# A decode state update in pairs on 32-row tiles of the matrix array

## The chip, the cores and the metric

The kernel runs on one core of one Trainium2 chip. The metric is the device time of one execution in microseconds (us). Engines: TensorE (PE; PEld is its weight load), VectorE (DVE), ScalarE (ACT), GpSimd (POOL), SyncE (SP).

## The reference

One layer of a hybrid decoder for a prompt of 256 tokens and for 8 decode sequences of 4 new tokens each (32 rows): 288 tokens in all, model width 2048. Around two large feed-forward parts (width 5632) stands a mixing part: one input projection, four mLSTM heads of width 256, a convolution group, one output projection. The decode sequences carry a state, a 256x256 matrix C per head and sequence:

```python
num = (jnp.einsum('bhls,bshd->blhd', s, vc)
       + jnp.einsum('blhd,bhde->blhe', qc, C) * w_inter.transpose(0, 2, 1)[..., None])
...
g_state = jnp.exp(bt[..., -1] + m - m_new)
g_keys = jnp.exp(bt[..., -1:] - bt + it - m_new[..., None])
C_new = g_state[..., None, None] * C + jnp.einsum('bhs,bshd,bshe->bhde', g_keys, kc, vc)
```

All data are float32. The change is about the second term of `C_new` for the 8 decode sequences ("batch elements"): a sum over only 4 tokens, for each of 4 heads.

## The kernel before

Everything is held feature-major: 128 features on the partitions, the 288 tokens in the free dimension. The weights come as 654 pieces of 128x1024 floats through four slots. Each piece is split into a rounded high half (`whi`, by ACT at L910) and a rest (`wlo`, by DVE at L1330 or POOL at L1860), and each 128x128 block of it makes three matmuls over 288 columns (L473 to L475). A piece is 8 blocks, so 24 matmuls; two pieces make an output tile of the input projection. Every engine runs a list of steps p, one for each piece of the mixing part, and the small work of the heads is hung onto these steps by hand: `head_part(h, k)` runs in step p = `KEYS_AT[h]` + k, with `KEYS_AT` = (8, 30, 54, 78), and on PE `between(p, j)` is called after block j of piece p. At even steps DVE first evicts a tile of the projection (`evict`, which waits for the end of a piece), then does the head parts, then its share of the splits.

What touches the change, for each head:

- ACT (k = 8) copies the 32 decode columns of K and V four times side by side (`kv4`), PE turns them to token-major (`to_token_major`), so 128 rows hold the 32 decode rows four times.
- The four copies carry the four products of two rounded halves each: ACT (k = 10) writes the high halves of `v4` and `k4`, DVE (k = 11, L1674 and L1678) turns some row groups into the rests. One 128-row matmul then adds high*high, high*rest, rest*high and rest*rest.
- ACT (k = 12, 13, L1189) writes `vm`, eight copies of `v4`, each with all rows but those of one batch element set to zero.
- `update_memory(h, b)` on PE makes, for one batch element, two matmuls (L744) of a 128x128 block of `k4` with the 256 columns of `vm[b]`, into bank 7 or 4 by turns. There are eight such places per head, three blocks apart, at `updates`, counted from step 16 + `LATE[h]`, with `LATE` = (2, 0, 0, 3).
- DVE (L1737) adds each result to the old state in `C`: batch elements 0 to 2 in step 16, 3 and 4 in step 17, 5 to 7 in step 18 (plus `LATE[h]`); the counter `cu_evicted` tells PE that a bank is free.
- `query_memory` (L705) reads the old states: it runs on 32-column tiles of the array, four batch elements beside one another. `token_columns` (L657) makes six matmuls over 36 rows.
- `attend` (L728) waits for DVE's L1717.

Of the kernel before, what the change touches and what calls it, by code (L numbers as in the profile page):

```python
# [29 lines left out]
P = 128  # L30
# [75 lines left out]
Q_GROUP = 4  # L106

# [67 lines left out]
def hybrid_layer_kernel(nc, stream, x_in, vecs, gate_w, gate_vec, c_in, n_in, conv_in,  # L175
                        y_out, cp_out, np_out, cs_out, ns_out, m_out, conv_out):
    with ExitStack() as ctx:
# [77 lines left out]
        vm = place("vm", [P, NB, DH], F32R)  # L255
# [8 lines left out]
        mask4 = place("mask4", [P, 4, NB], F32, prod_at)  # L264
# [8 lines left out]
        mask = place("mask", [P, NB])  # L273
# [9 lines left out]
        own = bass.AP(ident, 0, [[P, P], [Q_GROUP * NT, NB // Q_GROUP], [NS + NT, Q_GROUP], [1, NT]])  # L283
# [62 lines left out]
        cap_ready, cap_added = sem("cap_ready"), sem("cap_added")  # L346
        turn_ready, sums_ready = sem("turn_ready"), sem("sums_ready")
# [26 lines left out]
        def four(ap):  # L374

            return ap.unsqueeze(2).broadcast_to([P, DC, P // NS, NS])
# [79 lines left out]
        def _(pe):  # L456
# [237 lines left out]
            def query_memory(h):  # L694
# [7 lines left out]
                for r in range(NB // Q_GROUP):  # L702
                    for c in range(DC):
                        for j in range(Q_GROUP):
                            mm = pe.matmul(bank[4][NS * j:NS * (j + 1), 0:DH], qw[:, c, r, :],  # L705
                                           C[:, r * Q_GROUP + j, c, :], start=(r + c == 0),
                                           stop=(r == NB // Q_GROUP - 1 and c == DC - 1), skip_group_check=True,
                                           tile_position=(0, NS * j))
# [73 lines left out]
            updates = {(16, 1): 0, (16, 4): 1, (16, 7): 2, (17, 2): 3, (17, 5): 4, (18, 0): 5, (18, 3): 6, (18, 6): 7}  # L782

            def between(p, j):


                for h in range(H):
# [13 lines left out]
                    b = updates.get((k - LATE[h], j))  # L801
                    if b is not None:
                        update_memory(h, b)
# [98 lines left out]
        def _(act):  # L902
# [185 lines left out]
            def gate_rows():  # L1088

                act.wait_ge(args_ready, 1)  # L1090
                for k in range(2):
# [3 lines left out]
                act.activation(rowg[:, SEQ:SEQ + P].rearrange("h (j i) -> h j i", i=NS),  # L1095
                               g_arg[:, 0:NS].unsqueeze(1).broadcast_to([H, P // NS, NS]), ACT.Exp).then_inc(rows_ready, 1)
# [3 lines left out]
                act.dma_start(row_copy[:, R_GK:ROWS], rowg[:, 0:TOK]).then_inc(rows_stored, 16)  # L1100
# [25 lines left out]
            def head_part(h, k):  # L1126
# [9 lines left out]
                if h == 0 and k == 6:  # L1136

                    act.wait_ge(rows_stored, 32)
# [15 lines left out]
                if k == 8:  # L1154

                    act.wait_ge(tile_evicted, tile_of(h, "v1") + 1)
                    for n in range(2):
                        last = act.activation(kv4[:, n, :, :].rearrange("p c (j t) -> p c j t", j=P // NS),
                                              four(qkvo[:, 1 + n, :, SEQ:TOK]), ACT.Copy)
                    last.then_inc(kv4_ready, 1)  # L1160
                if k == 10:
# [8 lines left out]
                    act.activation(v4[:, :], bank[7][:, 0:DH], ACT.Copy, scale=col[:, 5, h:h + 1])  # L1170
                    act.activation(k4[:, :], bank[7][:, DH:2 * DH], ACT.Copy).then_inc(dec_hi, 1)
# [12 lines left out]
                if k in (12, 13):  # L1184
# [3 lines left out]
                    for b in range(4 * (k - 12), 4 * (k - 11)):  # L1188
                        act.activation(vm[:, b, :], v4[:, :].bitcast(F32), ACT.Copy, scale=mask[:, b:b + 1])\  # L1189
# [131 lines left out]
        def _(dve):  # L1321
# [238 lines left out]
            dve.tensor_reduce(mask[:, :], mask4[:, :, :].rearrange("p j b -> p b j"), AX_X, ALU.add)\  # L1560
# [33 lines left out]
            four_dec = [H, P // NS, NB, NT]  # L1594
# [573 lines left out]
```

## Time and profile before

| | |
|---|---|
| median of 3 runs | 2156.44 us (2156.44 to 2157.05) |
| the profiled execution | 2157.24 us |
| its span, first to last instruction | 2155.5 us |
| PE busy | 2149.3 us (100%), 16278 matmuls |
| DVE, ACT, POOL busy | 972.9, 895.1, 961.7 us |
| granted TensorE clock | 1.000 |

The span is 1.7 us short of the execution's own time. The busy time of an engine is the union of its instructions; the recorded duration of a matmul overlaps those of its neighbours, so the pace is read from starts, not from durations.

### The profile page before, as it was taken

How to read it: one execution, taken by the hardware profiler on the slowest of the kernel's cores; microseconds unless marked ns; L12 is line 12 of the kernel's file. 1: busy time of each engine (PE TensorE's matmuls, PEld its weight loads, DVE VectorE, ACT ScalarE, POOL GpSimd, SP SyncE). 2: the span in 40 equal slices, each digit the busy share in tenths (PEclk: the TensorE clock that was granted, in tenths of full speed). 3: DMA queues.
4: the chain of work that ended last, by engine and by line, in shares of the span. 5: the costliest groups of instructions: out<-in, count | busy, mean ns of one | idle time of the engine just before them, and what ended most of it. 6: DMA issues, size and time to landing. Idle time of an engine off the chain costs nothing.

```text
span 2155.5 us, 41798 instructions
## 1 busy us (share of the span) xinstructions
PE 2149.3 (100%) x16278; PEld 2138.5 (99%) x16278; DVE 972.9 (45%) x1406; ACT 895.1 (42%) x1159; POOL 961.7 (45%) x563
## 2 busy tenths in 40 slices
PE   9999999999999999999999999999999999999999
PEld 9999999999999999999999999999999999999998
DVE  6533432223434224987659738533432223333323
ACT  6434333333343335644345446433333333333443
POOL 1444443334444445466756332444443334444444
PEclk9999999999999999999999999999999999999999
DMA  7454555455555554656656544545455545554653
GB/s 249 165 168 163 165 166 172 159 165 168 167 164 162 170 169 146 208 191 229 239 191 226 194 160 148 172 160 171 156 172 168 167 157 170 162 172 157 210 164 129
DMA packets 104692, 376.63 MB, mean 175 GB/s; under 512 B 11640, under 2 KB 15868, under 8 KB 103584
## 3 DMA queue, kind: packets, MB, share of 16 engines
q1 hardware_dynamic: 97632, 349.00, 49.0%
q10 hardware_dynamic: 6848, 26.37, 3.5%
q8 instruction: 62, 1.02, 0.2%
q14 instruction: 22, 0.18, 0.0%
q0 software_dynamic: 128, 0.07, 0.0%
HBM read 360.21 MB, written 15.18 MB: 174 GB/s over the span
## 4 chain that ended last, share of the span: by engine, by line
PE 99%; DVE 1%; issue 0%; ACT 0%; POOL 0%; DVEq 0%; POOLq 0%
PE bank L475 30%; PE bank L473 30%; PE bank L474 30%; PE bank L528 1%; PE bank L535 1%; PE bank L539 1%; PE bank L833 1%; PE bank L835 1%; PE bank L834 1%; PE bank L546 0%; PE bank L744 0%; PE bank L770 0%; PE bank L687 0%; DVE wlo L1330 0%; DVE prod L1636 0%; PE bank L728 0%
## 5 line engine op out<-in xcount | busy, mean ns | idle before, releaser
L1860 POOL TENSOR_TENSOR wlo<-raw,whi 128x1024 fp32r<-128x1024 f32 x331 | 796.6, 2408 | 850.5 <-ACT whi L910 770.7
L473 PE MATMUL bank<-xh,whi 128*128 128x288 f32 x3344 | 992.1, 297 | 0.0
L474 PE MATMUL bank<-xl,whi 128*128 128x288 f32 x3344 | 988.3, 296 | 0.0
L475 PE MATMUL bank<-xh,wlo 128*128 128x288 f32 x3344 | 986.4, 295 | 0.0
L910 ACT ACTIVATE whi<-raw 128x1024 fp32r<-128x1024 f32 x652 | 687.3, 1056 | 604.8 <-PE bank L475 560.8
L1330 DVE TENSOR_TENSOR wlo<-raw,whi 128x1024 fp32r<-128x1024 f32 x323 | 467.7, 1449 | 771.2 <-ACT whi L910 769.9
L473 PEld LDWEIGHTS bank<-xh,whi 128*128 128x128 f32 x3344 | 630.2, 188 | 2.4 <-issue 2.2
L475 PEld LDWEIGHTS bank<-xh,wlo 128*128 128x128 f32 x3344 | 629.8, 188 | 0.0
L474 PEld LDWEIGHTS bank<-xl,whi 128*128 128x128 f32 x3344 | 628.7, 188 | 0.2
L475 PE MATMUL bank<-hh,wlo 128*128 128x288 f32 x1408 | 417.4, 296 | 0.0
L473 PE MATMUL bank<-hh,whi 128*128 128x288 f32 x1408 | 416.1, 296 | 0.0
L474 PE MATMUL bank<-hl,whi 128*128 128x288 f32 x1408 | 410.5, 292 | 0.0
L474 PEld LDWEIGHTS bank<-hl,whi 128*128 128x128 f32 x1408 | 268.4, 191 | 0.0
L473 PEld LDWEIGHTS bank<-hh,whi 128*128 128x128 f32 x1408 | 264.5, 188 | 0.0
L475 PEld LDWEIGHTS bank<-hh,wlo 128*128 128x128 f32 x1408 | 263.8, 187 | 0.0
L1883 POOL TENSOR_TENSOR scr<-scr 128x288 f32<-128x288 f32 x88 | 74.7, 849 | 208.7 <-ACT scr L999 208.7
L1003 ACT ACTIVATE hh<-scr 128x288 f32 (+1 forms) x88 | 39.1, 444 | 275.6 <-DVE scr L1468 275.6
L999 ACT ACTIVATE scr<-scr 128x288 f32<-128x288 f32 x88 | 39.2, 445 | 220.7 <-DVE scr L1447 220.7
L1447 DVE TENSOR_TENSOR scr<-bank,rstd 128x288 f32<-128x288 f32 x176 | 80.3, 456 | 77.1 <-PE bank L475 72.3
L1624 DVE SCALAR_TENSOR_TENSOR bank<-upad,vec,bank 128x256 f32<-128x256 f32 x232 | 92.8, 481 | 0.1
L1873 POOL TENSOR_TENSOR ssq<-ssq,sq 128x288 f32<-128x288 f32 x45 | 36.5, 812 | 79.3 <-ACT sq L1060 54.2
L1470 DVE TENSOR_TENSOR hl<-scr,hh 128x288 f32 (+1 forms) x88 | 40.3, 458 | 64.0 <-ACT hh L1003 64.0
(265 smaller groups left out, 1271.4 us busy)
## 6 DMA issues: line engine op xcount, KB each, us to landing
raw<-stream SPq DMA_DIRECT2D x654, 512.0 KB, 3.5
C<-c_in ACTq DMA_DIRECT2D x4, 2048.0 KB, 8.2
cs_out<-C ACTq DMA_DIRECT2D x4, 2048.0 KB, 7.9
late_kv<-late ACTq DMA_DIRECT2D x1, 2048.0 KB, 13.5
y_out<-x_res SPq DMA_DIRECT2D x7, 288.0 KB, 2.2
bc<-row_copy ACTq DMA_DIRECT2D x4, 448.0 KB, 8.6
conv_out<-upad ACTq DMA_DIRECT2D x4, 302.0 KB, 5.0
upad<-conv_in ACTq DMA_DIRECT2D x4, 272.0 KB, 3.4
```

What stands on the lines that cost most here:

```text
L473: pe.matmul(out, wh, mov_hi[:, k, :], start=first, stop=False)
L474: pe.matmul(out, wh, mov_lo[:, k, :], start=False, stop=False)
L475: return pe.matmul(out, wl, mov_hi[:, k, :], start=False, stop=last)
L910: act.activation(whi[:, g % SLOTS, :], raw[:, g % SLOTS, :], ACT.Copy).then_inc(hi_ready, 1)
L999: act.activation(scr[:, 2, :], scr[:, f % 2, :], ACT.Sigmoid).then_inc(sig_ready, 1)
L1003: act.activation(hh[:, k, :], scr[:, 4, :], ACT.Copy).then_inc(h_hi, 1)
L1330: dve.tensor_tensor(wlo[:, g % SLOTS, :], raw[:, g % SLOTS, :], whi[:, g % SLOTS, :].bitcast(F32), ALU.subtract).then_inc(lo_ready[g % SLO ...
L1447: ins = dve.tensor_tensor(out, src, rstd[:, :], ALU.mult)
L1470: dve.tensor_tensor(hl[:, k, :], scr[:, 4, :], hh[:, k, :].bitcast(F32), ALU.subtract)\
L1624: ins = dve.scalar_tensor_tensor(out=out, in0=up_prompt(j, SEQ, k), scalar=w, in1=acc, op0=ALU.mult, op1=ALU.add)
L1860: pool.tensor_tensor(wlo[:, g % SLOTS, :], raw[:, g % SLOTS, :], whi[:, g % SLOTS, :].bitcast(F32), ALU.subtract).then_inc(lo_ready[g % SL ...
L1883: pool.tensor_tensor(scr[:, 5 + f % 2, :], scr[:, f % 2, :], scr[:, 2, :], ALU.mult)\
```

## The change

The decode rows are ordered by batch element, then copy, then token: the 16 rows of a batch element (4 copies x 4 tokens) lie together, and a group of 32 rows holds two batch elements, 2g (even, r = 0) and 2g + 1 (odd, r = 1). The state update of a batch element then needs the 32 rows of its group only. `vm` has two versions, one with the odd and one with the even 16-row halves set to zero. Two batch elements of neighbouring groups (on different banks) are issued beside one another on 32-row tiles of the array, at four places per head.

```diff
+PAR = NB // Q_GROUP
+COPIES = P // NS
+UPDATE_ORDER = (0, 2, 1, 3, 4, 6, 5, 7)
...
-            def update_memory(h, b):
-
-                if b < 2:
-                    pe.wait_ge(den_ready if b == 0 else qc_evicted, h + 1)
+            def update_memory(h, n):
+
+                if n:
+                    pe.wait_ge(cu_evicted, NB * h + 2 * n)
                 else:
-                    pe.wait_ge(cu_evicted, NB * h + b - 1)
-                pe.wait_ge(vm_ready, NB * h + b + 1)
-                out = bank[4 if b % 2 else 7]
+                    pe.wait_ge(den_ready, h + 1)
+                    pe.wait_ge(qc_evicted, h + 1)
+                    pe.wait_ge(vm_ready, PAR * (h + 1))
                 for c in range(DC):
-                    mm = pe.matmul(out[:, c * DH:(c + 1) * DH], k4[:, c * P:(c + 1) * P], vm[:, b, :],
-                                   start=True, stop=True)
-                mm.then_inc(cu_done, 1)
+                    for b in UPDATE_ORDER[2 * n:2 * n + 2]:
+                        g, r = divmod(b, PAR)
+                        own_rows = slice(NS * g, NS * (g + 1))
+                        mm = pe.matmul(bank[4 if g % 2 else 7][:, c * DH:(c + 1) * DH], k4[own_rows, c * P:(c + 1) * P],
+                                       vm[own_rows, r, :], start=True, stop=True, tile_position=(NS * g, 0))
+                        if c == DC - 1:
+                            mm.then_inc(cu_done, 1)
...
-            updates = {(16, 1): 0, (16, 4): 1, (16, 7): 2, (17, 2): 3, (17, 5): 4, (18, 0): 5, (18, 3): 6, (18, 6): 7}
+            updates = {(16, 1): 0, (16, 7): 1, (17, 5): 2, (18, 3): 3}
...
-                act.dma_start(row_copy[:, R_GK:ROWS], rowg[:, 0:TOK]).then_inc(rows_stored, 16)
+                act.dma_start(row_copy[:, R_GK:R_GK + SEQ], rowg[:, 0:SEQ]).then_inc(rows_stored, 16)
+                act.dma_start(row_copy[:, R_GK + SEQ:ROWS].rearrange("h (b t) -> h b t", t=NT),
+                              in_copies(rowg[:, SEQ:SEQ + P])[:, :, 0, :]).then_inc(rows_stored, 16)
...
                     for n in range(2):
-                        last = act.activation(kv4[:, n, :, :].rearrange("p c (j t) -> p c j t", j=P // NS),
-                                              four(qkvo[:, 1 + n, :, SEQ:TOK]), ACT.Copy)
+                        for c in range(DC):
+                            last = act.activation(in_copies(kv4[:, n, c, :]), copied(
+                                qkvo[:, 1 + n, c, SEQ:TOK].rearrange("p (b t) -> p b t", t=NT)), ACT.Copy)
...
-                    act.activation(v4[:, :], bank[7][:, 0:DH], ACT.Copy, scale=col[:, 5, h:h + 1])
-                    act.activation(k4[:, :], bank[7][:, DH:2 * DH], ACT.Copy).then_inc(dec_hi, 1)
+                    act.wait_ge(colv_ready, 1)
+                    act.activation(v4[:, :], bank[7][:, 0:DH], ACT.Copy, scale=colv[:, 1, h:h + 1])
+                    act.activation(k4[:, :], bank[7][:, DH:2 * DH], ACT.Copy, scale=side[:, 1, 0:1]).then_inc(dec_hi, 1)
...
-                if k in (12, 13):
+                if k == 12:
...
-                    for b in range(4 * (k - 12), 4 * (k - 11)):
-                        act.activation(vm[:, b, :], v4[:, :].bitcast(F32), ACT.Copy, scale=mask[:, b:b + 1])\
+                    for r in range(PAR):
+                        act.activation(vm[:, r, :], v4[:, :].bitcast(F32), ACT.Copy, scale=mask[:, r:r + 1])\
                            .then_inc(vm_ready, 1)
...
+            dve.wait_ge(low_ready, 2)
+            dve.tensor_reduce(side[:, 0, 0:1], low16[:, :], AX_X, ALU.add)
+            link(dve.tensor_reduce(side[:, 0, 1:2], low8[:, :], AX_X, ALU.add))
+            dve.tensor_scalar(side[:, 1, :], side[:, 0, :], -2.0, 1.0, ALU.mult, ALU.add).then_inc(side_ready, 1)
...
+                    dve.wait_ge(side_ready, 1)
+                    for n in range(2):
+                        last = dve.tensor_scalar(colv[:, n, :], col[:, 5, :], side[:, n, 1:2], None, ALU.mult)
+                    last.then_inc(colv_ready, 1)
+                    dve.wait_ge(colv_ready, 1)
                 if k == 11:
 
                     dve.wait_ge(dec_hi, h + 1)
-                    for r in (NS, 3 * NS):
-                        dve.scalar_tensor_tensor(out=v4[r:r + NS, :], in0=bank[7][r:r + NS, 0:DH],
-                                                 scalar=col[r:r + NS, 5, h:h + 1], in1=v4[r:r + NS, :].bitcast(F32),
-                                                 op0=ALU.mult, op1=ALU.subtract)
-                    half = slice(2 * NS, P)
-                    dve.tensor_tensor(k4[half, :], bank[7][half, DH:2 * DH], k4[half, :].bitcast(F32), ALU.subtract)\
-                       .then_inc(dec_lo, 1)
+                    dve.scalar_tensor_tensor(out=v4[:, :], in0=bank[7][:, 0:DH], scalar=colv[:, 0, h:h + 1],
+                                             in1=v4[:, :].bitcast(F32), op0=ALU.mult, op1=ALU.add)
+                    dve.scalar_tensor_tensor(out=k4[:, :], in0=bank[7][:, DH:2 * DH], scalar=side[:, 0, 0:1],
+                                             in1=k4[:, :].bitcast(F32), op0=ALU.mult, op1=ALU.add).then_inc(dec_lo, 1)
...
-                for b in ((0, 1, 2), (3, 4), (5, 6, 7))[first] if 0 <= first < 3 else ():
-                    dve.wait_ge(cu_done, NB * h + b + 1)
-                    src = bank[4 if b % 2 else 7][:, :]
+                for n in ((0, 1), (2, 3), (4, 5, 6, 7))[first] if 0 <= first < 3 else ():
+                    dve.wait_ge(cu_done, NB * h + n + 1)
+                    b = UPDATE_ORDER[n]
+                    src = bank[4 if b // PAR % 2 else 7][:, :]
```

The new row order is carried through the rest: the masks (POOL's selects, two more memsets and four more selects for `low8` and `low16`, and DVE's three operations on `side` above), the layout of `own`, `cap` and `turn`, the choice of `C[:, PAR * j + r]` in `query_memory`, and DVE's query weights (k = 12), where the one multiply into `qw` becomes one for the even and one for the odd batch elements.

## Rows read from the trace of the kernel before

**Rows 1.** The page: busy time of the engines, granted clock, the chain that ended last

```profile
PE 2149.3 (100%) x16278; PEld 2138.5 (99%) x16278; DVE 972.9 (45%) x1406; ACT 895.1 (42%) x1159; POOL 961.7 (45%) x563
...
PEclk9999999999999999999999999999999999999999
...
PE 99%; DVE 1%; issue 0%; ACT 0%; POOL 0%; DVEq 0%; POOLq 0%
```

**Rows 2.** Instructions of L744: durations (min/median/max, ns), first and last start, shapes

```profile
L744 PE MATMUL bank<-vm,k x64: 274/279/285, 950.4 to 1214.4; 128*128 128x256 f32 x64
```

**Rows 3.** PE's timeline, second head: start, us, engine, line, shapes, count

```profile
1030.03 0.30 PE L473 MATMUL bank<-xh,whi 128*128 128x288 f32 x1
...
1030.43 0.39 PE L744 MATMUL bank<-vm,k 128*128 128x256 f32 x2
1030.66 0.29 PE L473 MATMUL bank<-xh,whi 128*128 128x288 f32 x1
...
1031.86 0.40 PE L744 MATMUL bank<-vm,k 128*128 128x256 f32 x2
```

**Rows 4.** Timeline of all engines around the column-tiled `query_memory`, first head

```profile
941.32 0.29 PE L475 MATMUL bank<-xh,wlo 128*128 128x288 f32 x1
941.54 1.93 PE L705 MATMUL bank<-C,qw 128*32 128x256 f32 x32
...
943.41 0.40 PE L473 MATMUL bank<-xh,whi 128*128 128x288 f32 x1
...
943.65 0.29 PE L474 MATMUL bank<-xl,whi 128*128 128x288 f32 x1
```

**Rows 5.** Timeline of all engines around the 36-row matmuls of `token_columns`

```profile
904.69 0.29 PE L475 MATMUL bank<-xh,wlo 128*128 128x288 f32 x1
...
904.91 0.74 PEld L657 LDWEIGHTS bank<-ident,both 36*128 36x128 f32 x6 [0.16 <-issue]
904.91 0.83 PE L657 MATMUL bank<-ident,both 36*128 36x8 f32 x6
...
905.67 0.40 PE L473 MATMUL bank<-xh,whi 128*128 128x288 f32 x1
...
905.91 0.29 PE L474 MATMUL bank<-xl,whi 128*128 128x288 f32 x1
```

**Rows 6.** Weight loads of one round of `query_memory` (PEld's timeline)

```profile
941.79 0.13 PEld L705 LDWEIGHTS bank<-C,qw 128*32 128x32 f32 x4
```

**Rows 7.** Timeline at the start of step 18, first head (piece starts at 957.19)

```profile
957.19 0.30 PE L473 MATMUL bank<-xh,whi 128*128 128x288 f32 x1
...
957.39 0.46 DVE L1540 TENSOR_TENSOR scr<-bank,rstd 128x288 f32<-128x288 f32 x1
```

**Rows 8.** Timelines of ACT, POOL and DVE before and in step 18, second head

```profile
1026.39 1.06 ACT L910 ACTIVATE whi<-raw 128x1024 fp32r<-128x1024 f32 x1 [0.84 <-PE bank L475]
...
1027.53 2.41 POOL L1860 TENSOR_TENSOR wlo<-raw,whi 128x1024 fp32r<-128x1024 f32 x1 [1.19 <-ACT whi L910]
...
1030.94 0.46 DVE L1525 TENSOR_TENSOR scr<-bank,rstd 128x288 f32<-128x288 f32 x1 [0.76 <-POOL upad L1995]
...
1031.32 0.74 DVE L1737 SCALAR_TENSOR_TENSOR C<-C,bc,bank 128x512 f32<-128x512 f32 x1
```

**Rows 9.** Timeline of a wait of PE for DVE, second head

```profile
1019.21 0.48 DVE L1717 SCALAR_TENSOR_TENSOR sq<-bank,turn,vs 128x256 f32<-128x256 f32 x1
...
1019.81 0.19 PEld L728 LDWEIGHTS bank<-st,vtok 128*128 128x128 f32 x1 [0.40 <-issue]
```

**Rows 10.** Groups by line and shape, 880 to 1260 us: count, busy us, mean ns, idle

```profile
L1189 ACT ACTIVATE vm<-v,mask 128x256 fp32r<-128x256 f32 x32 | 13.6, 495 | 1.8 <-DVE k L1678 1.8
...
L1687 DVE TENSOR_TENSOR qw<-qkvo,bc 128x64 f32<-128x64 f32 x4 | 2.5, 626 | 0.1
```

**Rows 11.** Timeline, first head: DVE's sums and PE's `denominators` that wait for them

```profile
935.18 0.18 DVE L1712 TENSOR_TENSOR scr<-bank,qwn 128x32 f32<-128x32 f32 x1
...
936.60 0.38 PE L716 MATMUL bank<-st,ones 128*128 128x128 f32 x2
```

More of the change, by code:

```diff
@@ L254, in hybrid_layer_kernel @@
         assert gwt_at + 4 * XC * GATE_M <= vm_at + 4 * NB * DH
-        vm = place("vm", [P, NB, DH], F32R)
+        vm = place("vm", [P, PAR, DH], F32R, vm_at)
+        low_at = gwt_at + 4 * XC * GATE_M
+        low8 = place("low8", [P, P // 8], F32, low_at)
+        low16 = place("low16", [P, P // 16], F32, low_at + 4 * P // 8)
+        assert low_at + 4 * (P // 8 + P // 16) <= vm_at + 4 * NB * DH
+        arena[0] += 4 * NB * DH
         late_kv = place("late_kv", [P, H, 4, DH], F32, xl_at)
@@ L263, in hybrid_layer_kernel @@
         assert upad_at + 4 * 7 * TOK <= arena[0]
-        mask4 = place("mask4", [P, 4, NB], F32, prod_at)
+        mask4 = place("mask4", [P, Q_GROUP, PAR], F32, prod_at)
         rows = place("rows", [H, R_GK], F32, prod_at)
@@ L272, in hybrid_layer_kernel @@
         ntmp = place("ntmp", [P, DC, NB])
-        mask = place("mask", [P, NB])
+        mask = place("mask", [P, PAR])
+        side = place("side", [P, 2, 2])
+        colv = place("colv", [P, 2, H])
         qwn = place("qwn", [P, DC, NS])
@@ L370, in compact, with copied, in_copies @@
             return row[:, SEQ:TOK].rearrange("h (b t) -> h b t", b=NB)
[L374 to L376 removed]
+        def copied(ap):
+            return ap.unsqueeze(2).broadcast_to([ap.shape[0], NB, COPIES, NT])
+        def in_copies(ap):
+            return ap.rearrange("p (b j t) -> p b j t", j=COPIES, t=NT)
         g_f, g_az, g_e, g_arg, g_wi = (gt[:, k, :] for k in range(5))
@@ L800, in between @@
                         attend(h)
-                    b = updates.get((k - LATE[h], j))
-                    if b is not None:
-                        update_memory(h, b)
+                    n = updates.get((k - LATE[h], j))
+                    if n is not None:
+                        update_memory(h, n)
                 if (p, j) == (MIX_FROM, 3):
@@ L1684, in head_part @@
                         dve.wait_ge(num_done, 3 * h)
[L1685 to L1694 removed]
+                    n = Q_GROUP * NT
+                    for r in range(PAR):
+                        w = bc[:, h % 2, R_WI:R_GK].rearrange("p (g r t) -> p r g t", r=PAR, t=NT)[:, r, :, :].unsqueeze(1)
+                        last = dve.tensor_tensor(
+                            qw[:, :, r, n * r:n * (r + 1)].rearrange("p c (g t) -> p c g t", t=NT),
+                            qkvo[:, 0, :, SEQ:TOK].rearrange("p c (g r t) -> p c r g t", r=PAR, t=NT)[:, :, r, :, :],
+                            w.broadcast_to([P, DC, Q_GROUP, NT]), ALU.mult)
+                    link(last)
+                    for r in range(PAR):
+                        old = n0[:, h, :, :].rearrange("p c (g r) -> p c r g", r=PAR)[:, :, r, :].unsqueeze(3)\
+                            .broadcast_to([P, DC, Q_GROUP, NT])
+                        last = dve.tensor_tensor(
+                            qwn[:, :, :].rearrange("p c (g r t) -> p c r g t", r=PAR, t=NT)[:, :, r, :, :],
+                            qw[:, :, r, n * r:n * (r + 1)].rearrange("p c (g t) -> p c g t", t=NT), old, ALU.mult)
                     link(last)
@@ L1980, in _ @@
                     pool.wait_ge(pool_chain, 4)
+            for low, n in ((low8, 4), (low16, 8)):
+                pool.memset(low[:, :], 1.0).then_inc(pool_chain, 1)
+            pool.wait_ge(pool_chain, 6)
+            for low, n in ((low8, 4), (low16, 8)):
+                pool.affine_select(out=low[:, :], in_=low[:, :], compare_op=ALU.is_ge, fill=0.0, base=-n,
+                                   pattern=[[-2 * n, P // (2 * n)]], channel_multiplier=1).then_inc(pool_chain, 1)
+            pool.wait_ge(pool_chain, 8)
+            for low, n in ((low8, 4), (low16, 8)):
+                pool.affine_select(out=low[:, :], in_=low[:, :], compare_op=ALU.is_ge, fill=0.0, base=2 * n - 1,
+                                   pattern=[[2 * n, P // (2 * n)]], channel_multiplier=-1).then_inc(low_ready, 1)
             pool.wait_ge(xsq_sum, 2)
```

52 lines of the change are left out of this document (21 added, 31 removed).

## The prediction

> **What bounds the kernel now.** I read the page first: PE is busy in 2149.3 us of the 2155.5 us span, every slice has the full granted clock (the 2.4 GHz level), and the chain that ended last is PE for 99% [rows 1]. So a nanosecond taken from PE's list is a nanosecond of the end, one that PE waits is one too, and work taken from ACT, DVE or POOL counts only where PE waits for it. The view by line then shows what the change rebuilds: 64 matmuls of L744, 256 columns each [rows 2]. Their recorded duration, 0.28 us, is not their price: neighbours overlap. The price is read from starts: L744's pair starts at 1030.43 and the next block at 1030.66, while one block of three matmuls takes ((1031.86 - 1030.43) - 0.24) / 3 = 0.395 us [rows 3]. So a place costs 0.24 us, and all 32 places 32 x 0.24 = 7.7 us. That is all the change can save on PE, 3.8 us if every two matmuls run in the time of one: 0.18% of the kernel, under the 0.2% (4.3 us) that a measurement can tell from no change.
>
> **What a place costs after.** Four matmuls stand in one place: two rounds of two tiles. At best that is 2 x 0.12 + 0.01 = 0.25 us. But these are 32-row tiles between full-array matmuls, and two views show what such a stretch costs. `query_memory` runs on 32-column tiles: from L475's start at 941.32 to its first matmul at 941.54 it takes 0.22 us where full matmuls follow one another after 0.13, and behind it L473 holds 0.24 instead of 0.13 until L474 starts [rows 4]. The 36-row matmuls of L657, a part of the rows as in the change, show the same two numbers, 0.22 and 0.24 [rows 5]. I read it so: PE runs empty (0.09), only then loads weights, so a load that otherwise lies under the matmul before it stands in the open (0.11 for 128 columns: L657's six loads lie (0.74 - 0.19) / 5 = 0.11 apart), and the same twice at the exit. The test is the whole of L705: 0.09 + 0.03 for its first 32-column load + eight rounds + 0.02 + 0.09 + 0.11. A round is (1.93 - 0.38) / 7 = 0.22 us, with the last matmul's duration of 0.38 taken off, so 2.1 us; measured from 941.32 to 943.65, less the two ordinary spacings of 0.13, it is 2.07 [rows 4].
>
> So a new place is 0.09 (empty) + 0.11 (first weights) + 0.24 (two rounds; the second's weights load under the first) + 0.01 (second tile) + 0.09 (empty) + 0.11 (the next block's weights) = 0.65 us. Sixteen places make 10.4 us against 7.7 us: 2.7 us more. The lower bound is 16 x 0.25 = 4.0 us, so 3.7 less, if row tiles cost no change-over at all; I take the other end because both kinds of part-array work on record pay it. Whether the two tiles' loads run side by side no row shows for row tiles: for column tiles four loads lie within 0.13 - 0.11 = 0.02 us [rows 6], so I take them as parallel; one behind the other is a rival below.
>
> The Trainium skill speaks against this change in TensorEngine Tiling (Array Packing), section Key Properties: changing the tiling mode, not just the tile, drains TensorE. By that rule each of the 16 places pays a drain at both ends; the 0.09 us at each end agrees with it [rows 4, 5].
>
> **A new wait.** Each place fills both banks, so PE at place n waits until 2n results are added by DVE. The places at (16,7) and (17,5) are six blocks (2.4 us) behind the one before, and it takes 0.09 + 0.11 + 0.12 to the second round, 0.28 for its matmul [rows 2], and 1.4 us for DVE's two additions (below), 2.0 us in all: covered. The place at (18,3) is not: it needs six additions, but the fifth and sixth are in DVE's step 18, and there DVE first evicts a projection tile that ends with the piece. In the first head the piece starts at 957.19, the eviction at 957.39 (0.20 later) [rows 7]; the next operation follows after 0.38 (1030.94 to 1031.32), an addition takes 0.75 and two in a row 0.68 + 0.75 [rows 8]; and a load on PE starts 0.12 after the DVE operation it waits for ends (1019.69 to 1019.81) [rows 9]. That is 0.20 + 0.38 + 0.68 + 0.75 + 0.12 = 2.13 us after the piece started; PE comes after four blocks, 1.58. The 0.09 in which PE runs empty passes meanwhile: 2.13 - 1.58 - 0.09 = 0.46 us. Nothing is queued before it that could go ahead: every main matmul behind it waits too.
>
> In the second and third head the eviction starts 0.91 after the piece (1030.03 to 1030.94), because POOL's gating multiply is late; POOL hangs on ACT's split at 1026.39, released by the end of the piece two before [rows 3, 8]. One new place (0.65) lies before that point where two old ones (0.48) lay: POOL comes 0.17 later. The start of the piece moves by 3 x 0.65 - 5 x 0.24 = 0.75. So the lag is 0.91 + 0.17 - 0.75 = 0.33 instead of 0.20, and the wait 0.59. The bounds are 0.46 and, with the lag unmoved, 1.2. The fourth head's step 18 lies behind the projection and has no eviction ahead: no wait. Together 0.46 + 2 x 0.59 = 1.6 us.
>
> **What lies beside.** ACT makes 8 `vm` copies instead of 32, 24 x 13.6 / 32 = 10 us less [rows 10], and 16 narrower copies instead of 8; DVE makes two rests per head instead of three, two small multiplies and three reductions or scalings once; POOL two memsets and four selects, before its splits and while it waits. One more small store goes out on ACT's queue two steps before the rows are read back, and only late work, eight pieces ahead, waits for it. None of these engines sets the end; I take 0. The closest is DVE in the first head, without a gap until its sums end at 935.36; `denominators` comes at 936.60 [rows 11]. Cover: 1.24 us. The multiply into `qw` becomes two, and the mean of 626 ns for 64 columns [rows 10], beside 0.18 us for 32 columns in L1712 [rows 11], says that it sometimes stands behind something else. If the second one stands as long as a whole POOL split (2.41 [rows 8]), PE waits 2.4 - 1.2 = 1.2 us; once, in this head. I take 0 (two multiplies without a link between them pass together), and keep 1.2 for the range.
>
> **Sum.** +2.7 + 1.6 = +4.3 us on the profiled 2157.24 us (span 2155.5 and 1.7 around it), which lies 0.8 us above the median. On the median 2156.44: 2160.7 us, just at the 0.2%.
>
> **Rivals.** *Loads one behind the other* (slower): the four loads of a place take 0.11 each in the open; place 0.09 + 4 x 0.11 + 0.12 + 0.09 + 0.11 = 0.85 us, 16 of them 13.6, +5.9; the piece moves more (1.35), so the waits are 0.46 each, +1.4; 2163.7 us. For: L657's loads do queue at 0.11 [rows 5], though on one tile. Against: rows 6. It decides as soon as a load on the second tile starts 0.1 us after the first.
> *No change-over for row tiles* (not slower): places 4.0 us, -3.7; but PE then comes earlier to (18,3): lag 0.91 - 0.23 + 0.45 = 1.13, wait 1.48 twice and 0.55 once, +3.5; 2156.2 us. Against: rows 5. Without the waits too it would be 2152.7, still within 0.2%.
> The Trainium skill, TensorE: Matmul & The Clock Gate, Part 3, gives a packed set one matmul's time and about 4 ns per further tile; by that alone a round costs what it does in this rival. L705's rounds agree with it; its ends don't.
> *The wait at (18,3) is hidden*, if DVE evicts sooner than read: 2159.1 us. Against: rows 7 and 8 leave it 0.55 us too late.
>
> **Chances.** The forecast 0.56, half of it on either side of the bound; loads in a row 0.18; no change-over 0.10; hidden wait 0.10; others 0.06. Slower: 0.28 + 0.18 + 0.03 = 0.49. Same: 0.28 + 0.20 = 0.48. Faster 0.03, since no case worked out reaches it. The range 2157.0 to 2164.0 holds the forecast with 1.2 us for DVE or for late POOL, hidden waits and queued loads; it leaves out the 0.10 and the others.
>
> **What would show it.** Right: L744's successor in 16 places of four matmuls, each entered 0.22 us after the last L475 and left with 0.24 between L473 and L474; PE waiting for L1737's successor three times, at the last place of heads one to three, about half a microsecond each. Wrong: weight loads 0.11 apart on two tiles; starts of 0.13 at the entry; a wait at `denominators` in the first head; or a matmul on 32 rows that is slower than one on 128.

## The result, and the profile after

| | before | after |
|---|---|---|
| median (18 runs each) | 2156.65 us (2156.10 to 2157.21) | 2160.74 us (2160.38 to 2161.39) |
| the profiled execution, its span | 2157.24, 2155.5 us | 2161.22, 2159.5 us |
| PE busy | 2149.3 us | 2152.0 us |
| granted TensorE clock | 1.000 | 1.000 |

The change makes the kernel 4.1 us slower: ratio 1.0019, 95% interval [1.0013, 1.0026]. The interval leaves out 1, so the loss is real; its middle lies just under the 0.2% bound and its upper end above it.

The lines of the page that answer to [rows 1], from the kernel after (L488 to L490 are the main matmuls now, L762 the state update):

```profile
PE 2152.0 (100%) x16278; PEld 2136.1 (99%) x16278; DVE 974.3 (45%) x1411; ACT 887.1 (41%) x1143; POOL 961.8 (45%) x569
...
PEclk9999999999999999999999999999999999999999
...
PE 96%; DVE 2%; issue 1%; POOL 1%; ACT 0%; POOLq 0%; DVEq 0%; ACTq 0%
```

The clock is whole in every slice, as before, so no time is the clock's. ACT has 8 us less to do, and nothing comes of it. In the chain that ended last PE's share has fallen from 99% to 96%, and DVE's and POOL's have risen (1% to 2%, 0% to 1%): PE waits for them somewhere. The view of waits says where (engine, what it was to do, for whom it waited: total us, times, longest), PE of the kernel after:

```profile
PE bank L561 <- POOL ident L1965: 1.7, 1, 1.7
PE bank L762 <- DVE C L1769: 1.1, 3, 0.4
PE bank L743 <- DVE sq L1748: 0.4, 2, 0.2
PE bank L789 <- ACT rpost L1333: 0.2, 1, 0.2
PE bank L684 <- ACT cpr L1180: 0.2, 1, 0.2
```

The first, third and fourth stand in the same view of before too, with the same times. New are three waits at the update's last place (L762), which the prediction has, and one at `to_token_major` (L684), which it doesn't have.

A place of the update, in PE's timeline of the kernel after (answers to [rows 3]):

```profile
953.50 0.29 PE L490 MATMUL bank<-xh,wlo 128*128 128x288 f32 x1
953.73 0.50 PE L762 MATMUL bank<-vm,k 32*128 32x256 f32 x4
954.16 0.40 PE L488 MATMUL bank<-xh,whi 128*128 128x288 f32 x1
954.40 0.29 PE L489 MATMUL bank<-xl,whi 128*128 128x288 f32 x1
```

Read it by starts, as L705 was read in the prediction: from the last L490 to L489 behind the place it is 954.40 - 953.50 = 0.90 us (unrounded 0.893), less two ordinary spacings of 0.13 (together 0.263) is 0.63. The entry takes 0.23 (unrounded 0.224) and L488 holds 0.24: both numbers of [rows 4, 5]. All 16 places without their waits cost 0.62 to 0.63, mean 0.629.

The three waits, the one in the second head in DVE's and PE's timeline of the kernel after (its piece starts at 1031.86, answers to [rows 8]):

```profile
1032.20 0.46 DVE L1548 TENSOR_TENSOR scr<-bank,rstd 128x288 f32<-128x288 f32 x1 [2.77 <-POOL upad L2038]
1032.58 1.39 DVE L1769 SCALAR_TENSOR_TENSOR C<-C,bc,bank 128x512 f32<-128x512 f32 x2
```

```profile
1033.32 0.29 PE L490 MATMUL bank<-xh,wlo 128*128 128x288 f32 x1
1034.03 0.50 PE L762 MATMUL bank<-vm,k 32*128 32x256 f32 x4 [0.41 <-DVE C L1769]
```

DVE evicts 0.34 after the piece starts and is done with two additions at 1033.97; PE starts 0.06 later, 0.71 after its last L490 instead of 0.22. Over the three heads these places cost 0.981, 1.109 and 1.147 us, 0.35 + 0.48 + 0.52 = 1.35 above 0.629.

The fourth wait, in the first head. The chain that ended last, of the kernel after, from 903 to 918 us (start us, us, what):

```profile
909.58 2.44 DVE colv L1697
...
912.04 3.23 DVE bank L1649 x8
915.27 0.37 DVE qkvo L1557
...
915.88 0.70 ACT cpr L1180 x3
916.58 0.04 issue
916.62 0.66 PE bank L684 x4
```

A multiply of 128x4 numbers, new with the change (`colv`), takes 2.44 us there. The timelines of DVE and then POOL in the kernel after show beside what:

```profile
908.19 0.17 DVE L1692 COPY col<-bank 128x24 f32<-128x24 f32 x1
908.40 3.60 DVE L1697 TENSOR_SCALAR colv<-col,side 128x4 f32<-128x4 f32 x2
912.04 3.23 DVE L1649 SCALAR_TENSOR_TENSOR bank<-upad,vec,bank 128x256 f32<-128x256 f32 x8
915.18 0.45 DVE L1557 TENSOR_TENSOR qkvo<-bank,rstd 128x288 f32<-128x288 f32 x1
```

```profile
904.90 7.08 POOL L1892 TENSOR_TENSOR wlo<-raw,whi 128x1024 fp32r<-128x1024 f32 x3 [1.14 <-ACT whi L929]
```

POOL's three splits stand one behind the other until 911.98; DVE's two multiplies end at 912.00. Behind them come eight convolution steps and then the eviction of V (L1557 at 915.18, 3.46 us later than in the kernel before), ACT's copies `kv4` (which the trace calls `cpr`) and PE's L684. In DVE's timeline before:

```profile
911.72 0.45 DVE L1534 TENSOR_TENSOR qkvo<-bank,rstd 128x288 f32<-128x288 f32 x1
```

The place of L684 costs 1.242 us where the same place cost 0.875 before, 0.37 more.

So the 4.1 us are: places 16 x 0.629 - 32 x 0.236 = 2.5; waits at L762 1.35; L684 0.37; sum 4.2. Measured independently, by how far the main matmuls (288 columns each, counted through) start later than their counterparts in before: -0.16 us ahead of the mixing part (at 857.6) and +3.97 behind it (at 1217.1), so 4.13 us, all of it in the mixing part; behind 1217 us the shift stays at 3.97. "Shift" below means this difference. (The starts of a program's first 60 us differ from execution to execution by up to 1.2 us, so shifts are finer than times here.)

### The profile page after: what moved, and what is told of

Same layout as the page of the kernel before. It is cut to its first block, busy times and chain, and to the rows that moved or that the text cites. A ratio compares the mean times of both kernels' runs of the same rounds, so it can differ in the third digit from the quotient of the medians.

```text
span 2159.5 us, 41763 instructions
## 1 busy us (share of the span) xinstructions
PE 2152.0 (100%) x16278; PEld 2136.1 (99%) x16278; DVE 974.3 (45%) x1411; ACT 887.1 (41%) x1143; POOL 961.8 (45%) x569
## 4 chain that ended last, share of the span: by engine, by line
PE 96%; DVE 2%; issue 1%; POOL 1%; ACT 0%; POOLq 0%; DVEq 0%; ACTq 0%
PE bank L490 29%; PE bank L488 29%; PE bank L489 29%; PE bank L543 1%; PE bank L554 1%; PE bank L550 1%; PE bank L852 1%; PE bank L854 1%; PE bank L853 1%; DVE bank L1649 0%; POOL wlo L1892 0%; PE bank L561 0%; PE bank L789 0%; PE bank L702 0%; DVE wlo L1353 0%
## 5 line engine op out<-in xcount | busy, mean ns | idle before, releaser
L488 PE MATMUL bank<-xh,whi 128*128 128x288 f32 x3344 | 993.4, 297 | 0.0
L489 PE MATMUL bank<-xl,whi 128*128 128x288 f32 x3344 | 988.3, 296 | 0.0
L490 PE MATMUL bank<-xh,wlo 128*128 128x288 f32 x3344 | 986.4, 295 | 0.0
L488 PEld LDWEIGHTS bank<-xh,whi 128*128 128x128 f32 x3344 | 630.2, 188 | 4.0 <-issue 2.2
L490 PEld LDWEIGHTS bank<-xh,wlo 128*128 128x128 f32 x3344 | 629.7, 188 | 0.0
L489 PEld LDWEIGHTS bank<-xl,whi 128*128 128x128 f32 x3344 | 628.7, 188 | 0.2
L490 PE MATMUL bank<-hh,wlo 128*128 128x288 f32 x1408 | 417.4, 296 | 0.0
L488 PE MATMUL bank<-hh,whi 128*128 128x288 f32 x1408 | 416.1, 296 | 0.0
L489 PE MATMUL bank<-hl,whi 128*128 128x288 f32 x1408 | 410.5, 292 | 0.0
L489 PEld LDWEIGHTS bank<-hl,whi 128*128 128x128 f32 x1408 | 268.4, 191 | 0.0
L488 PEld LDWEIGHTS bank<-hh,whi 128*128 128x128 f32 x1408 | 264.5, 188 | 0.0
L490 PEld LDWEIGHTS bank<-hh,wlo 128*128 128x128 f32 x1408 | 263.8, 187 | 0.0
```

Source lines behind the costliest of these rows:

```text
L488: pe.matmul(out, wh, mov_hi[:, k, :], start=first, stop=False)
L489: pe.matmul(out, wh, mov_lo[:, k, :], start=False, stop=False)
L490: return pe.matmul(out, wl, mov_hi[:, k, :], start=False, stop=last)
```

## The experiments

**The timetable alone.** Kernel before, with the four places of the change, two batch elements in each, on the whole array:

```diff
-            updates = {(16, 1): 0, (16, 4): 1, (16, 7): 2, (17, 2): 3, (17, 5): 4, (18, 0): 5, (18, 3): 6, (18, 6): 7}
+            updates = {(16, 1): 0, (16, 7): 1, (17, 5): 2, (18, 3): 3}
...
-                for b in ((0, 1, 2), (3, 4), (5, 6, 7))[first] if 0 <= first < 3 else ():
+                for b in ((0, 1), (2, 3), (4, 5, 6, 7))[first] if 0 <= first < 3 else ():
```

> The kernel before, full-array matmuls and all, but with the new timetable: two batch elements at each of four places per head, into banks 7 and 4 at once, and DVE's additions in groups of 2, 2 and 4. Theory (the tiles cost 2.5 us and the new timetable's wait at the last place of heads one to three costs the rest): a place of four full matmuls takes 4 x 0.118 = 0.47 us, so places cost nothing more than before; PE still waits for the fifth and sixth addition. The wait measured after the change was the lag of the eviction plus 0.24 us; here the lag is 0.20 in the first head and about 0.7 in the next two (the piece moves by 0.23 only), so 0.4 + 0.9 + 0.9 us, and some 0.1 each for a weight load in the open: +2.3 to +2.5, 2159.0 us. Rival (all of the loss is the tiles', the timetable costs nothing): 2156.6 us. Rival (the timetable is all of it): 2160.7 us.

Measured: 2158.79 us, ratio 1.0011 [1.0002, 1.0019], shift +2.5. A place of four whole-array matmuls costs 0.475, twice 0.24, so the places cost nothing more; the whole 2.5 are waits. The first row of PE's waits, and one of the three in its timeline:

```profile
PE bank L745 <- DVE C L1739: 1.8, 3, 0.7
```

```profile
1031.74 0.29 PE L475 MATMUL bank<-xh,wlo 128*128 128x288 f32 x1
1032.78 0.74 PE L745 MATMUL bank<-vm,k 128*128 128x256 f32 x4 [0.74 <-DVE C L1739]
```

They are longer than in the change (0.74 against 0.41), as the prediction's way of counting the lag has it: its piece starts at 1030.29 and DVE evicts at 1030.96, a lag of 0.67, and 0.91 - (3 x 0.475 - 5 x 0.236) is 0.67. Places of 0.475 move the piece less than places of 0.63 do.

**The tiles alone.** The change, with DVE's fifth and sixth addition in step 17 instead of behind the eviction of step 18:

```diff
-                for n in ((0, 1), (2, 3), (4, 5, 6, 7))[first] if 0 <= first < 3 else ():
+                for n in ((0, 1), (2, 3, 4, 5), (6, 7))[first] if 0 <= first < 3 else ():
```

> The changed kernel with one edit: DVE adds the fifth and sixth result in step 17, ahead of the eviction of the projection tile, instead of behind it in step 18. Theory: the three waits at the place (18,3), 1.35 us together in the changed kernel, go; a place stays 0.63 us; 2159.4 us. Rival (the wait only moves: the eviction, now behind two more additions, is late for PE or for POOL): 2160.7 us, with a new wait of PE elsewhere.

Measured: 2159.67 us, ratio 1.0015 [1.0006, 1.0024], shift +2.9. The three waits at L762 are gone, and all 16 places cost 0.62 to 0.63. DVE itself now waits for PE's places 15 times instead of 12 (17.3 us in the mixing part instead of 10.5) and no longer for POOL at that eviction, but no new wait of PE comes of it. The wait of L684 stays. It was then taken out too, by an edit told below, in one kernel with both:

> The changed kernel with both repairs: DVE's fifth and sixth addition in step 17, and colv from the accumulator bank. Theory: what is left against the kernel before is the tiles alone, 16 x 0.63 - 32 x 0.236 = +2.5 us, and the wait at denominators in the first head that showed when to_token_major's went (0.27 us): 2159.3 us, and slower than before by its whole interval. Rival (the waits were the loss, tiles cost nothing): 2156.6 us.

Measured: 2159.56 us, ratio 1.0014 [1.0005, 1.0023], shift +2.44 (-1.24 to +1.20). PE's waits, whole:

```profile
PE bank L561 <- POOL ident L1965: 1.7, 1, 1.7
PE bank L743 <- DVE sq L1748: 0.4, 2, 0.2
PE bank L789 <- ACT rpost L1333: 0.2, 1, 0.2
```

These are before's. What is left in this profile is the places, 2.5 us: two row tiles with their change-over against two whole-array places. The median is 3.1 above before's, 0.6 more than this shift. The profiled execution was the fastest of the eleven (2158.43 to 2160.01); the others may have a wait at `denominators` as told below (0.17 to 0.46 us), which would be a part of it, but no profile of them shows it.

**What a place consists of.** The change, with each place's two rounds written twice (the second time the same results again):

```diff
-                for c in range(DC):
+                for m, c in enumerate((0, 1, 0, 1)):
...
-                        if c == DC - 1:
+                        if m == 3:
```

> The changed kernel with each round of a place done twice (the second pair of rounds writes the same results again): eight matmuls on two tiles per place instead of four. Theory (two tiles run side by side, weight loads too, and a place has a fixed price of about 0.40 us for running empty and loading in the open, twice): each further round is 0.11 to 0.12, a place 0.63 + 0.23 = 0.86 us, 16 x 0.23 = +3.7 us against the changed kernel, 0.3 less for waits that PE now comes later to: 2164.1 us. Rival (weight loads of the two tiles one behind the other): a round is 0.22, +7.0 us, 2167.7 us. Rival (the price of a place is in its matmuls, with no fixed part): a place doubles, 1.26 us, +10 us, 2170.7 us.

Measured: 2165.70 us, ratio 1.0043 [1.0030, 1.0056]. PE's timeline:

```profile
953.39 0.29 PE L490 MATMUL bank<-xh,wlo 128*128 128x288 f32 x1
953.61 0.74 PE L762 MATMUL bank<-vm,k 32*128 32x256 f32 x8
954.28 0.40 PE L488 MATMUL bank<-xh,whi 128*128 128x288 f32 x1
954.51 0.29 PE L489 MATMUL bank<-xl,whi 128*128 128x288 f32 x1
```

A place costs 0.865 (954.51 - 953.39 less 0.26), 0.237 more for two rounds of two matmuls each: a round of two tiles costs 0.118, one matmul's time. So the rest, 0.629 - 0.237 = 0.39 us, is paid once for each place whatever stands in it. The shift is 3.5 above the change's, as expected. The time is 5.0 above it. In the profile this execution is 0.5 us ahead of the change's up to the mixing part, so the last work of every engine ends 3.0 later; but the span ends 4.8 later, and the medians say that this is no accident of one execution. The other 1.8 us are the last two stores: from issue to landing they take 4.8 us (L446) and 4.5 (L1329), against 2.9 and 2.7 in the change. On one of the two queues of instructions the page counts one packet of 16 KB more than the change's page; the change's row, then this run's:

```profile
q8 instruction: 62, 1.02, 0.2%
```

```profile
q8 instruction: 63, 1.03, 0.2%
```

The last one here starts at 2160.93, among those stores, and takes 0.88 us; the change's last starts at 2140.24. That this packet holds the stores up is likely, but no run takes it away.

**Whether the tiles run side by side.** The change, with each tile's two matmuls listed together:

```diff
-                for c in range(DC):
-                    for b in UPDATE_ORDER[2 * n:2 * n + 2]:
+                for b in UPDATE_ORDER[2 * n:2 * n + 2]:
+                    for c in range(DC):
...
-                        if c == DC - 1:
-                            mm.then_inc(cu_done, 1)
+                    mm.then_inc(cu_done, 1)
```

> The changed kernel with the four matmuls of a place issued tile by tile (both halves of one batch element, then both of the other) instead of by turns. Theory (two tiles run side by side only when neighbours in PE's list lie on different tiles): first matmul alone, second and third together, fourth alone, so three rounds instead of two; a place goes from 0.63 to 0.74 us, 16 x 0.118 = +1.9 us against the changed kernel, 0.1 to 0.2 less for waits: 2162.5 us. Rival (side by side gives nothing, the places are bound by weight loads): 2160.7 us. Rival (PE reorders freely): 2160.7 us, with the same starts as in the changed kernel.

Measured: 2160.90 us, ratio 1.0020 [1.0011, 1.0030]; its shift is 0.25 above the change's, which is this profile's wait at L731 (below). A place costs 0.63 as before the edit. Starts of the single records of one place, in us, the loads on the first line of each pair:

```
the change     953.726 953.729 953.834 953.837   then L488 954.161
               953.727 953.731 953.949 953.954
tile by tile   953.760 953.766 953.868 953.875   then L488 954.198
               953.761 953.768 953.985 953.991
four tiles     950.761 950.765 950.768 950.771 950.870 950.873 950.876 950.880   then L496 951.203
               950.763 950.766 950.770 950.773 950.986 950.990 950.992 950.996
```

In the change two tiles' loads start 3 ns apart, not 0.11: the rival of loads one behind the other is out. In the edited list the second matmul belongs to the tile that is busy, and still a matmul starts 7 ns after the first, and two more 0.22 later. A record doesn't name its row tile, but it has the count that the matmul adds to `cu_done`. In the edited list the second and the fourth matmul count; in the records of all 16 places it is the third and the fourth. So the first matmuls of both tiles ran ahead of both second ones, and the place takes two rounds, 0.63 us, where the order of the list would take three, 0.75. My theory fell: the matmul that had to wait was passed over, and the other tile's was taken. Whether PE turned them round or the step that makes the program out of the kernel, no record tells. (The Trainium skill, TensorE: Matmul & The Clock Gate, Part 3, has matmuls start strictly in the order of the program; if the list reached PE as the kernel has it, the measurement differs from it, and decides.)

**The small multiplies.** The change, with the two `colv` multiplies reading their column from PSUM, where it stands anyway, ahead of its copy:

```diff
-                        last = dve.tensor_scalar(colv[:, n, :], col[:, 5, :], side[:, n, 1:2], None, ALU.mult)
+                        last = dve.tensor_scalar(colv[:, n, :], bank[7][:, 5 * H:6 * H], side[:, n, 1:2], None, ALU.mult)
```

> The changed kernel with DVE's two small multiplies into colv reading the accumulator bank instead of SBUF, and done ahead of the copy into col. Theory: in the changed kernel they took 3.60 us, where such an operation takes 0.15, because they stood behind POOL's splits; that made the last eviction of V 3.4 us late in the first head, and PE waited 0.37 us for kv4 in to_token_major. With an operand in PSUM they don't stand behind POOL: both take under 0.4 us, PE enters to_token_major after 0.13 us, 2160.4 us. Rival (the reductions into side or the four narrower copies are what is late): the wait of 0.37 us stays, 2160.7 us.

Measured: 2160.89 us, ratio 1.0020 [1.0011, 1.0028]: the same as the change; the 0.4 us that were to go did not. DVE's timeline, then POOL's, then PE's:

```profile
907.97 0.34 DVE L1694 TENSOR_SCALAR colv<-bank,side 128x4 f32<-128x4 f32 x2
...
926.16 3.85 DVE L1715 TENSOR_TENSOR qw<-qkvo,bc 128x32 f32<-128x32 f32 x2
930.04 2.39 DVE L1723 TENSOR_TENSOR qwn<-qw,n 128x32 f32<-128x32 f32 x2
```

```profile
904.67 7.10 POOL L1892 TENSOR_TENSOR wlo<-raw,whi 128x1024 fp32r<-128x1024 f32 x3 [1.12 <-ACT whi L929]
...
925.21 7.06 POOL L1892 TENSOR_TENSOR wlo<-raw,whi 128x1024 fp32r<-128x1024 f32 x3
```

```profile
936.38 0.46 PE L731 MATMUL bank<-st,ones 128*128 128x128 f32 x2
```

The pair takes 0.34 us instead of 3.60, beside the same three splits of POOL (904.67 to 911.77), and L684 costs 0.875 again, as before the change. But here the two `qw` multiplies and the two `qwn` behind them, which read SBUF alone, stand behind POOL's splits (which end near 927.6, 929.9 and 932.3; DVE's pairs end at 930.01 and 932.43), and PE waits at `denominators` (L731): the place costs 0.762 us against 0.492 without a wait, so 0.27 of the 0.37 is gone again.

The rule behind both: the Trainium skill, SBUF — State Buffer, Who interferes with whom, says that VectorE and GpSimd share a pair of SBUF ports which one instruction holds to its end; a DVE instruction with two SBUF inputs, or a copy or multiply by a scalar in a two-port mode, waits for the running GpSimd one, and one with at most one SBUF input outside those modes does not. The rows agree: 3.60 us with SBUF operands, ending with POOL's split, 0.34 with PSUM; in which mode the multiply ran no row shows.

**Whether the late rows make the wait at `denominators`.** The `colv` edit alone doesn't make that wait: the kernel with both edits contains it, and its place at L731 costs 0.493, without a wait. The wait comes where POOL's splits fall late, and POOL's order there begins when the gate rows land. The change stores its last rows with a scattered read (every fourth group of 4 values); in this edit ACT writes them once more, contiguous, and the store reads that:

```diff
+                act.activation(g_f[:, 0:NS], g_arg[:, 0:NS], ACT.Exp).then_inc(rows_ready, 1)
...
-                act.dma_start(row_copy[:, R_GK + SEQ:ROWS].rearrange("h (b t) -> h b t", t=NT),
-                              in_copies(rowg[:, SEQ:SEQ + P])[:, :, 0, :]).then_inc(rows_stored, 16)
+                act.dma_start(row_copy[:, R_GK + SEQ:ROWS], g_f[:, 0:NS]).then_inc(rows_stored, 16)
```

> The changed kernel with one edit: its third row store reads a contiguous copy of the 32 values instead of every fourth group of the 128. Theory: the scattered store is what makes the gate rows land late. In the seven profiles with it, POOL's first use of the rows starts 18.1 to 19.2 us ahead of the place of denominators in the first head (waits there taken off), mean 18.7; in the four without it 19.0 to 20.0, mean 19.6. So here about 19.6 us and no wait at denominators; the time is 2160.6 us, the same as the change, because the profile of the change has no such wait to win. Rival: the landing time scatters by itself, and the interval lies anywhere between 18.1 and 20.0.

> The same kernel as the run before, a second profile: theory 19.0 to 20.0 us from the rows' first use to the place of denominators, rival anywhere between 18.1 and 20.0 us.

> The change itself, unedited, a second profile: theory 18.1 to 19.2 us from the rows' first use to the place of denominators; rival 18.1 to 20.0 us. Both: the wait of to_token_major in the first head (0.35 to 0.4 us) is there again, and the three waits at the last update places.

Measured: 2160.95 us, 4.4 above the median of before beside it (2156.56); a further execution of it 2160.57, of the change 2160.63. The intervals in us, from the start of POOL's first use of the rows to that of `denominators`, less PE's wait there, sorted over all profiles:

```
one store (before, timetable alone)          19.7 20.0                                   no wait at denominators
contiguous third store (4 profiles)          19.0 19.4 19.8 20.3                         no wait
scattered third store (8 profiles)           18.1 18.2 18.5 18.6 18.6 19.0 19.1 19.2     waits in the first five
```

The theory holds in the main: the mean is 18.6 us with the scattered store and 19.6 with the contiguous one, though the two sets meet at 19.0 to 19.2, and the 20.3 lies above the range that was expected. The landing itself keeps them apart: from the issue of the read-back (L1145 in the change) the rows take 12.9 to 13.8 us in the eight profiles with the scattered store, 11.9 to 12.8 in the four with the contiguous one, 12.0 and 12.3 with one store. The load of `C`, issued right behind the stores, is late too (8.9 to 9.2 us against 8.2 to 8.5 with the contiguous store), so it is not the rows alone; why, no run shows. In the five profiles with 18.6 us or less PE waits at `denominators`, 0.17 to 0.46 us. Between the medians of the change and of this edit that doesn't show. The wait at L684 stands in all seven profiles in which `colv` is worked out from SBUF (0.35 to 0.43 us by starts; the view of waits lists it in five of them) and in none of the five with PSUM. The second profile of the change has the three waits at L762 again.

**Fewer change-overs.** If a place's stretch of row tiles costs 0.39 whatever stands in it, four tiles in two places should cost less than two in four. In heads one to three, all four row groups run beside one another, into banks 7, 4 and two banks that the projection has free there; the fourth head keeps its pairs; `colv` as above:

```diff
-UPDATE_ORDER = (0, 2, 1, 3, 4, 6, 5, 7)
+UPDATE_ORDER = {False: (0, 2, 1, 3, 4, 6, 5, 7), True: (0, 2, 4, 6, 1, 3, 5, 7)}
...
+            wide_updates = {(16, 1): 0, (17, 5): 1}
...
+                groups = ((0, 1), (2, 3), (4, 5, 6, 7)) if h == H - 1 else ((0, 1, 2, 3), (), (4, 5, 6, 7))
```

> The changed kernel with colv from the accumulator bank and, in heads one to three, four batch elements side by side on all four row tiles: two places per head instead of four, the two further results in two banks of the projection that stand empty there; head four unchanged. Theory (a place has a fixed price of about 0.40 us and each round 0.118, whatever the number of tiles): a place of four tiles costs 0.64 us, 6 x 0.64 + 4 x 0.63 = 6.4 us against 7.6 us of the kernel before; no place waits, 0.3 us of wait at denominators stays: -0.9 us, 2155.7 us. Rival (four tiles share the load path or the way to the banks): a place 0.8 us or more, 2156.7 us or slower. Rival (the borrowed banks are late for the next projection tile): a wait of PE at the start of a tile, about 0.5 us each, six times, 2159 us.

Measured: 2155.76 us, ratio 0.9996 [0.9987, 1.0005], shift -0.82. A place of eight matmuls in PE's timeline, and the one new wait:

```profile
950.54 0.29 PE L498 MATMUL bank<-xh,wlo 128*128 128x288 f32 x1
950.76 0.51 PE L772 MATMUL bank<-vm,k 32*128 32x256 f32 x8
951.20 0.40 PE L496 MATMUL bank<-xh,whi 128*128 128x288 f32 x1
951.44 0.30 PE L497 MATMUL bank<-xl,whi 128*128 128x288 f32 x1
```

```profile
PE bank L739 <- DVE scr L1757: 0.2, 1, 0.2
```

The place costs 0.641, 0.01 more than with four matmuls; its first four loads start within 10 ns (list above). With the contiguous store as well:

> As the kernel with four tiles, and the small third store of the gate rows comes from a contiguous copy (one more ScalarE operation of 0.2 us) instead of 32 runs of 16 bytes. Theory (the scattered store makes the rows come back about 0.7 us later in the first head, POOL's splits with them, and DVE's small multiplies stand behind these): the rows land earlier, the wait at denominators goes, 2155.4 us. Rival (it is the third store as such, or the start of the large state load behind it): the rows land as late as in the kernel with four tiles, 2155.7 us.

Measured: 2155.21 us, ratio 0.9995 [0.9986, 1.0004], shift -1.32; the wait at `denominators` is gone. POOL's first use of the rows in the run before it and in this one:

```profile
918.30 0.25 POOL L2070 TENSOR_TENSOR wt<-bc,cap 128x32 f32<-128x32 f32 x1 [2.26 <-DMA bc<-row_copy]
```

```profile
915.91 0.26 POOL L2070 TENSOR_TENSOR wt<-bc,cap 128x32 f32<-128x32 f32 x1 [0.86 <-DMA bc<-row_copy]
```

The places account for it: 6 x 0.641 + 4 x 0.629 = 6.4 against 7.6, -1.2. Last, an edit beside the change, on the two waits of `attend` that before has too ([rows 9]): DVE's eviction of the queries ahead of the normaliser and split work of step 14.

```diff
+                if k == 14 and h < H - 1:
+                    conv_decode(h)
-                if k == (16 if late else 15):
+                if k == (16 if late else 14):
...
-                if k == 14 and h < H - 1:
-                    conv_decode(h)
```

> Four tiles per place and the row store from a contiguous copy, as in the run before, and DVE's eviction of the queries moved ahead of the normaliser and split work of step 14 in the second and third head, where attend stands waiting for it twice on PE. Theory: those waits are each some 0.43 us with the weight load that lies open behind them, nothing else comes late, and the mixing part gets 0.8 to 0.9 us shorter than in the run before: about 2154.4 us, or 2.1 us under the kernel before, still about 0.1% and within what a measurement can tell. Rival: the wait only moves to the work that the eviction now stands ahead of (the denominators or a split of the same step), and the time stays at 2155.2 us.

Measured: 2154.49 us, ratio 0.9990 [0.9981, 0.9999], shift -2.21, 0.89 below that of the run before. PE's waits, whole:

```profile
PE bank L569 <- POOL ident L1980: 1.7, 1, 1.7
PE bank L799 <- ACT rpost L1347: 0.2, 1, 0.2
```

Both lie outside the mixing part, where the view has no wait of PE left. This kernel is faster than both kernels, than before by 2.0 us or 0.09%: well under the bound of 0.2%, with an interval that only just leaves out 1. Of the shift 1.2 are the tiles' places.

## Why the prediction was right

2160.7 us were forecast and 2160.74 measured. That they agree this closely is luck: the forecast adds 4.3 to a median of 3 runs, 2156.44, while over 18 runs before has 2156.65 and the change adds 4.1. The terms of the sum, one by one:

- *A place, 0.65.* Measured 0.629, +2.5 instead of +2.7. Its make-up holds: entry 0.22, exit 0.24; the two change-overs with their open loads 0.392, for which the prediction has 0.40 (0.09 + 0.11, twice), and two rounds of two tiles 0.237, for which it has 0.25. No run separates the 0.09 from the 0.11. That a round takes 0.12 was a guess that came true: no row of row tiles stood behind it, and L705's rounds of four column tiles, which the prediction says agree with one matmul's time, take 0.22 [rows 4].
- *The loads run side by side.* Right: 3 ns apart.
- *The waits, 0.46 + 0.59 + 0.59 = 1.6.* Right in place, number and cause; 0.35, 0.48 and 0.52 measured. The lag in the second head was to be 0.33 and is 0.34. Mis-sized is the end: PE started 0.06 after DVE's second addition, not 0.12 as taken from [rows 9], and the two additions took 1.39, not 1.43.
- *What lies beside, 0.* This term failed, by 0.37 us. The prediction saw the mechanism, a small DVE operation that stands for as long as a POOL split, but looked for it at the multiply that the change splits in two (`qw`, at `denominators`), not at the two that it adds (`colv`), and named their cost nowhere; their place in the first head is followed within 8 us by a PE step that waits for DVE. It also let the added store pass because only late work waits for the rows; the rows do land later, by about 1.0 us, and of the 1.24 us of cover at `denominators` 0.50 are left in the change's profile (DVE's last sum ends at 936.27, PE comes at 936.77), nothing in five of the eight profiles with that store. One of the five is the second profile of the change itself, with a wait of 0.17 there: the sign of being wrong that the prediction names.
- *Errors that cancel.* Places 0.2 and waits 0.25 too dear, 0.37 missed: the sum is 0.1 off, better than its parts.

The rivals are out: loads in a row by the 3 ns, no change-over by the 0.39 us, the hidden wait by the three waits seen.

## What to carry to other kernels

Row tiles between whole-array matmuls pay a fixed toll for each stretch, here 0.39 us, and 0.118 a round of 256 columns after that; four tiles beside one another cost 0.01 more than two. So count stretches first, and fill each one with all four row groups before splitting it: two tiles in 16 stretches lost 2.5 us, four in 6 and two in 4 won 1.2. A timetable that puts work for two buffers into one place also doubles what must be drained ahead of the next: look at what the draining engine does in between, since moving two additions one step was worth 1.2 us here. And on DVE a multiply of four columns is not free: with its operands in SBUF it took here what was left of POOL's running instruction, with its input in PSUM it did not.

## What the hardware showed that was not expected

- A matmul on a free row tile starts ahead of one listed earlier for a busy tile (7 ns after the first; the place stays at 0.63 us); what turned them round, no record tells.
- Four row tiles' weight loads start within 10 ns, and a place with eight matmuls costs 0.01 more than one with four.
- Two 128x4 multiplies on DVE take 3.60 us with SBUF operands beside POOL's splits, 0.34 with one operand in PSUM.
- Behind a store of 32 values a row that reads them in groups of 4, the read-back of the rows takes 12.9 to 13.8 us from issue to landing, behind one from contiguous columns 11.9 to 12.8.
